# Value tiles with the tokens stationary, convolutions read from the accumulator banks, and modulation steps in other turns

## The reference

```python
h = modulate(layer_norm(x), sh1, sc1)            # sh1, sc1, ... from silu(cond) @ w_ada + b_ada
proj = h @ p['w_in']                             # columns: pool 512 | q 512 | k 512 | v 512 | o 512 | gates 16
qk = silu(dwconv1d_centred(concat([q, k]), w_qk_conv))   # x[t-1]*w0 + x[t]*w1 + x[t+1]*w2, per column
h_f, h_b = mlstm_chunkwise(...)                  # needs q, k by columns and v by tokens
pool_out = pool_mixer(xp, w_pool, pool_scale)    # window means over the grid, then a 128x128 product per group
mix = concat([pool_out, ml_out]) @ p['w_out']
```

## Time and profile before

| | |
|---|---|
| median of three runs | 1317.82 us |
| the profiled execution | 1317.26 us, its span 1315.5 us |
| TensorE busy | 1261.0 us (96%) |
| VectorE / GpSimd busy | 1035.2 us / 668.4 us |
| mean granted TensorE clock | 0.994 of full speed |
| units 4 to 31 | 88.1 to 289.8 us of the span |

### The profile page before, as it was taken

How to read it: one execution, slowest core, us unless ns; L and a number is a source line. 1 busy time by engine, 2 the same in 40 slices (tenths; PEclk the granted TensorE clock), 3 DMA queues, 4 the chain that set the end, 5 groups by cost and what they waited for, 6 DMA issues and landing times.

```text
span 1315.5 us, 21778 instructions
## 1 busy us (share of the span) xinstructions
PE 1261.0 (96%) x7739; PEld 1156.9 (88%) x7739; DVE 1035.2 (79%) x1506; ACT 592.9 (45%) x1029; POOL 668.4 (51%) x503
## 2 busy tenths in 40 slices
PE   6999999999998899989999999999999999999996
PEld 2589999999987778888999999999999988888885
DVE  6455899894567688879887878787875779888898
ACT  5732224545445734555444444444443455345430
POOL 1001999744343011329888888788877874200011
PEclk9999999999999999999999999999999999999999
DMA  9532332473225532203363535444543679945892
GB/s 359 157 88 84 90 94 67 136 240 81 81 81 192 192 113 97 80 33 106 99 204 129 175 120 196 137 160 141 179 147 133 199 238 366 355 134 188 293 322 108
DMA packets 164851, 210.28 MB, mean 160 GB/s; under 512 B 10567, under 2 KB 102819, under 8 KB 164515
## 3 DMA queue, kind: packets, MB, share of 16 engines
q1 hardware_dynamic: 164286, 204.47, 47.4%
q0 software_dynamic: 288, 4.72, 0.9%
q10 hardware_dynamic: 197, 0.06, 0.0%
HBM read 161.49 MB, written 47.72 MB: 159 GB/s over the span
## 4 chain that ended last, share of the span: by engine, by line
PE 51%; POOL 2%; DVE 1%; issue 1%; ACT 0%; POOLq 0%
PE ps L1609 11%; PE ps L1607 11%; PE ps L1608 11%; PE ps L1640 6%; PE ps L1642 6%; PE ps L1641 6%; POOL tlo L2264 0%; POOL ulo L2264 0%; POOL xlo L2264 0%; POOL dwlo L2264 0%; POOL xwlo L2264 0%; PE ps L1166 0%; POOL wsum L2465 0%; DVE z L3275 0%; DVE z L3274 0%
## 5 line engine op out<-in xcount | busy, mean ns | idle before, releaser
L3089 DVE SCALAR_TENSOR_TENSOR ps<-gs,taps,ps 128x945 f32<-128x945 f32 (+2 forms) x176 | 215.7, 1226 | 10.0 <-ACT ps L2042 4.6
L2407 POOL TENSOR_TENSOR rstd<-mv,neghalf 128x1 f32<-128x1 f32 x27 | 25.1, 928 | 258.2 <-DVE mv L3266 156.9
L1259 PE MATMUL ps<-h1hi,whi 128*128 128x384 f32 x432 | 152.9, 354 | 2.7 <-DVE wlo L2603 2.7
L1259 PE MATMUL ps<-h1lo,whi 128*128 128x384 f32 x432 | 145.2, 336 | 0.0
L1259 PE MATMUL ps<-h1hi,wlo 128*128 128x384 f32 x432 | 145.1, 336 | 0.0
L1640 PE MATMUL ps<-dwhi,uhi 128*128 128x512 f32 x290 | 113.1, 390 | 1.3 <-POOL dwlo L2264 1.3
L1642 PE MATMUL ps<-dwhi,ulo 128*128 128x512 f32 x290 | 112.9, 389 | 0.0
L1641 PE MATMUL ps<-dwlo,uhi 128*128 128x512 f32 x290 | 112.8, 389 | 0.0
L1607 PE MATMUL ps<-thi,xhi 128*128 128x288 f32 x320 | 94.3, 295 | 2.0 <-issue 1.1
L2264 POOL TENSOR_TENSOR wlo<-raw,whi 128x512 fp32r<-128x512 f32 x44 | 61.9, 1408 | 65.4 <-ACT whi L1712 29.7
L1609 PE MATMUL ps<-thi,wlo 128*128 128x288 f32 x320 | 94.4, 295 | 0.0
(11 more groups left out here) (444 smaller groups left out, 3998.8 us busy)
## 6 DMA issues: line engine op xcount, KB each, us to landing
raw<-in_w_up SPq DMA_DIRECT2D x78, 256.0 KB, 4.7
u_rows<-val SPq DMA_DIRECT2D x22, 576.0 KB, 2.9
adaw<-in_w_ada SPq DMA_DIRECT2D x24, 512.0 KB, 4.0
st<-in_w_down SPq DMA_DIRECT2D x22, 512.0 KB, 4.3
t_rows<-st SPq DMA_DIRECT2D x11, 1024.0 KB, 4.6
raw<-in_w_in SPq DMA_DIRECT2D x40, 256.0 KB, 4.4
w_raw<-in_w_down SPq DMA_DIRECT2D x33, 256.0 KB, 5.3
v_raw<-u_rows SPq DMA_DIRECT2D x33, 256.0 KB, 4.8
```

The source lines that it names most:

```text
L1259: last = mm(ps[:, bank, 0:GN], a[:, n % 2, k * P:(k + 1) * P], b[:, kk, grp(g)], start=(kk == 0 and a is whi and b is h1hi), stop=(kk == K ...
L2407: tt(rstd[:, j % 4, :], mv[:, j % 4, 1:2], neghalf[:, 0, :], ALU.pow).then_inc(rstd_ready, 1)
L3089: step(stt(a3[:, ro, co], g3[:, ri, ci], taps[:, tap:tap + 1], a3[:, ro, co], ALU.mult, ALU.add), 2 + m)
```

## The change

- **Value tiles.** Units 8 to 15 are replaced by nine `v_tile`s, one for each chunk of 128 tokens. The token chunk is now the stationary operand and the 512 value columns move: 24 matmuls of 128x512 for each tile, in one bank. The result has tokens on its partitions, so the transposes are gone, and ScalarE's `v_evac` copies 9 tiles of 512 columns. Unit 8+k is now the 128 input rows k of the value weights. All eight have to be split before the first value tile can end, into buffers of their own (`vw`), so their loads, `hi` and `lo` are moved ahead, into turns 4 to 8. `lo(16)` and `lo(17)` are made in turn 10.
- **Convolutions.** ScalarE makes only the scaled copy into `qk`. VectorE reads the two outer taps' input straight from the banks. A convolution is in two halves of four instructions, half 0 in odd turns and half 1 in the even turn after it. From unit 20 on TensorE waits for `conv_done` (both halves) before it begins the tile that takes these banks.
- **Modulation steps** are spread differently over the turns: from turn 7 to 15 there are 17 instead of 13, in turns 20 to 23 one each instead of none, in turns 24 to 30 ten instead of eighteen. The third and later `ada2_cols` come three units behind their last step instead of two.

The diff, cut to its core (the memory places of `vw`, counts of `tile_out` and the regrouping of `jobs_after` are left out):

```diff
+V_FIRST, V_LAST = 2 * H, 4 * H
+LO_TURN = {4: (6,), 5: (7,), 6: (8, 9, 10), 7: (11, 12, 13), 8: (14, 15), 10: (16, 17)}
 ...
-ADA_UNITS = {4: 2, 6: 2, 7: 1, 8: 1, 9: 2, 10: 2, 11: 1, 12: 2, 13: 1, 14: 2, 15: 1, 16: 2, 17: 1, 18: 1, 19: 1,
-             24: 2, 25: 3, 26: 3, 27: 3, 28: 3, 29: 3, 30: 1}
+ADA_UNITS = {4: 2, 6: 2, 7: 2, 8: 1, 9: 2, 10: 2, 11: 2, 12: 2, 13: 2, 14: 2, 15: 2, 16: 2, 17: 1, 18: 1, 19: 1,
+             20: 1, 21: 1, 22: 1, 23: 1, 24: 1, 25: 1, 26: 2, 27: 2, 28: 2, 29: 1, 30: 1}
 ...
-ADA_COLS = {min(...) + 2: j for j in range(N_ADA2)}
-for _n in range(12):
-    JOBS[10 + _n] = ("v", _n // 3, _n % 3)
+ADA_COLS = {min(...) + (2 if j < ADA_SIDE[0] - 1 else 3): j for j in range(N_ADA2)}
 ...
# SyncE: loads
+                if V_FIRST <= n < V_LAST:
+                    k = n - V_FIRST
+                    sp.dma_start(raw[:, n % RAWN, :], w_in[0, k * P:(k + 1) * P, 3 * H * P:4 * H * P]).then_inc(raw_in[n % RAWN], 16)
+                    return
 ...
-                if n + RAWN < U_OUT:
-                    load_proj(n + RAWN)
+                for unit in {4: (8,), 5: (9, 10), 6: (11, 12), 7: (13, 14, 15), 8: (16, 17), 9: (18, 19)}.get(n, () if RAWN < n < V_LAST else (n + RAWN,)):
+                    if unit < U_OUT:
+                        load_proj(unit)
 ...
# TensorE: value tiles in place of units 8 to 15
-            def misc_job(job):
-                _, h, part = job
-                ...
-                    last = nc.tensor.transpose(ps[:, 7, (ck % 4) * P:(ck % 4 + 1) * P], qk[:, h, chunk(ck)], ident[:, :])
+            def v_tile(t, between=None):
+                if t == 0:
+                    pe.wait_ge(tile_out, tile_count(2))
+                elif t == NG:
+                    pe.wait_ge(tile_out, tile_count(3))
+                elif t >= 2 * NG:
+                    pe.wait_ge(v_ready, t - 2 * NG + 1)
+                for k in range(KT):
+                    if t == 0:
+                        wait_lo(pe, V_FIRST + k)
+                    w_hi, w_lo = [x[:, :] for x in vw[k]]
+                    for a, w in ((h1hi, w_hi), (h1hi, w_lo), (h1lo, w_hi)):
+                        last = mm(ps[:, t % (2 * NG), :], a[:, k, chunk(t)], w,
+                                  start=(k == 0 and a is h1hi and w is w_hi), stop=(k == KT - 1 and a is h1lo))
+                    if t == NT - 1:
+                        last.then_inc(pe_unit, 1)
+                    if between is not None and k in (2, 5):
+                        between(k // 3)
+                if t < NT - 1:
+                    last.then_inc(pe_v, 1)
 ...
             for n in range(4, 2 * NPROJ):
                 tile, bank = n // 2, 3 * ((n // 2) % 2)
+                if V_FIRST <= n < V_LAST:
+                    v_tile(n - V_FIRST, lambda g: jobs_after(n, g))
+                    jobs_after(n, NG - 1)
+                    if n == V_LAST - 1:
+                        v_tile(NT - 1)
+                    continue
                 wait_lo(pe, n)
-                if n % 2 == 0:
-                    pe.wait_ge(tile_out, tile - 1)
+                if n % 2 == 0 and n > V_LAST + 2:
+                    pe.wait_ge(conv_done, tile - 2 * H - 1)
 ...
# ScalarE
+            def v_evac(t):
+                ...
+                fn(v1[:, t, :, 0:P], ps[:, t % (2 * NG), :].rearrange("p (h n) -> p h n", h=H), ACT.Copy).then_inc(v_ready, 1)
 ...
-                hi(n + 2)
+                if n < V_FIRST - 2:
+                    hi(n + 2)
+                elif n < V_FIRST:
+                    for unit in LO_TURN[n] + ((14, 15) if n == 7 else ()):
+                        v_hi(unit)
 ...
-                        fn(qk[:, j, :]..., ps[:, b0:b0 + 3, 0:GN], ACT.Copy, scale=...)
-                    fn(dst..., ps[:, b0:b0 + 3, 0:GN], ACT.Copy).then_inc(tile_out, 1)
+                    dst, scale = (qk[:, H + tile, :], 1.0) if tile < H else (qk[:, j, :], colv[:, V_CONV + KT + j:V_CONV + KT + j + 1])
+                    fn(dst..., ps[:, b0:b0 + 3, 0:GN], ACT.Copy, scale=scale).then_inc(tile_out, 1)
 ...
# VectorE
-            def conv(j):
-                src, dst = work[:, tile % 2, :], qk[:, j, :]
-                ...
-                        last = stt(dst[:, o], src[:, i_], w[a], dst[:, o], ALU.mult, ALU.add)
+            def conv(j, half):
+                tile = 2 * H + j
+                b0 = 3 * (tile % 2)
+                dst, cut = qk[:, j, :].rearrange("p (g n) -> p g n", g=NG), LAT - 2 * GN
+                if half == 0:
+                    dve.wait_ge(tile_out, tile_count(tile))
+                ...
+                for out, src in ((dst[:, 0:2, to:to + GN - 1], ps[:, b0:b0 + 2, at:at + GN - 1]),
+                                 (dst[:, 2, to:to + cut - 1], ps[:, b0 + 2, at:at + cut - 1]),
+                                 (dst[:, 2, cut + to:GN - 1 + to], ps[:, b0 + 2, cut + at:GN - 1 + at]), joints):
+                    last = stt(out, src, w, out, ALU.mult, ALU.add)
+                if half == 0:
+                    link(last)
                 else:
+                    last.then_inc(conv_done, 1)
 ...
-                if n + 2 < U_LO:
-                    lo(n + 2)
+                for unit in LO_TURN.get(n, () if n < V_LAST else (n + 2,)):
+                    if unit < U_LO:
+                        lo(unit)
 ...
-                if n % 2 == 0 and n // 2 > 2 * H:
-                    conv(n // 2 - 1 - 2 * H)
-            conv(2 * H - 1)
+                if n > V_LAST:
+                    conv((n - 1) // 2 - 2 * H, (n + 1) % 2)
+            conv(2 * H - 1, 1)
```

More of the change, by code:

```diff
@@ L106 @@
 assert ada_done(2 * NPROJ) == N_ADA2 * KT
-ADA_COLS = {min(n for n in range(3, 2 * NPROJ) if ada_done(n) >= KT * (j + 1)) + 2: j for j in range(N_ADA2)}
-for _n in range(12):
-    JOBS[10 + _n] = ("v", _n // 3, _n % 3)
+ADA_COLS = {min(n for n in range(3, 2 * NPROJ) if ada_done(n) >= KT * (j + 1)) + (2 if j < ADA_SIDE[0] - 1 else 3): j
+            for j in range(N_ADA2)}
 POOL_FIRST = 24
@@ L344, in first_split, with tile_count @@
             return wearly[:, 2 * n - 4, :], wearly[:, 2 * n - 3, :]
+        vw = [(place(f"vwhi{k}", [P, UC], at, F32R), place(f"vwlo{k}", [P, UC], at + 4 * UC, F32R))
+              for k, at in enumerate([qk_at + 8 * UC * k for k in range(4)] + [work_at + 1024 + 8 * UC * k for k in range(2)])]
+        late_at = work_at + 4 * 2 * T + 4 * H * P
+        vw += [(place("vwhi6", [P, UC], late_at, F32R), place("vwlo6", [P, UC], late_at + 4 * UC, F32R)),
+               (place("vwhi7", [P, UC], late_at + 8 * UC, F32R), place("vwlo7", [P, UC], past_gates, F32R))]
+        assert late_at + 12 * UC <= work_at + 16 * T and past_gates + 4 * UC <= M0
+        assert 16 * UC * 2 <= 4 * H * T and 1024 + 16 * UC <= 8 * T
+        def tile_count(tile):
+            return tile + 1 if tile < H else tile + 1 - H
         def xslot(n):
@@ L1283, in gate_job @@
                     mm(ps[:, 7, 3 * P:4 * P], bc(gcol[:, 4:5], [P, P]), ident[:, :], start=True, stop=True).then_inc(pe_tok, 1)
-            def misc_job(job):
-                _, h, part = job
[L1288 to L1292, removed]
-                    last = nc.tensor.transpose(ps[:, 7, (ck % 4) * P:(ck % 4 + 1) * P], qk[:, h, chunk(ck)], ident[:, :])
-                last.then_inc(pe_v, 1)
-                jobs_done["v"] += 1
+            def v_tile(t, between=None):
[18 more added lines that the diff above has]
+                    last.then_inc(pe_v, 1)
             def pool_job(j):
                 g, part = divmod(j, 3)
-                pe.wait_ge(v_ready, 13)
+                pe.wait_ge(tok_ready, 1)
                 pe.wait_ge(wpl_in, 16)
@@ L1307, in _, with jobs_after @@
             gate_transposes()
+            def jobs_after(n, g):
+                if g == 1 and n in ADA_COLS:
+                    if n > POOL_FIRST:
+                        pe.wait_ge(po_ready, min(2 * (n - POOL_FIRST), 12))
+                    ada2_cols(ADA_COLS[n])
+                if (n, g) in GATE_JOBS:
+                    gate_job(GATE_JOBS[n, g])
             for n in range(4, 2 * NPROJ):
                 tile, bank = n // 2, 3 * ((n // 2) % 2)
+                if V_FIRST <= n < V_LAST:
[4 more added lines that the diff above has]
+                    continue
                 wait_lo(pe, n)
-                if n % 2 == 0:
-                    pe.wait_ge(tile_out, tile - 1)
+                if n % 2 == 0 and n > V_LAST + 2:
+                    pe.wait_ge(conv_done, tile - 2 * H - 1)
+                elif n == V_FIRST - 2 or n == V_FIRST - 4:
+                    pe.wait_ge(tile_out, tile_count(tile - 2))
                 for g in range(NG):
+                    if n == V_LAST:
+                        pe.wait_ge(v_ready, 2 * NG + g + 1)
                     last = proj_group(n, bank + g, g)
@@ L1316, in _ @@
                         last.then_inc(pe_unit, 1)
[L1317 to L1322 removed]
+                    jobs_after(n, g)
                     if g == 0 and POOL_FIRST <= n < POOL_LAST:
```

(8 more changed lines are left out.)

92 lines of the change are left out of this document (39 added, 53 removed).

## The result

The changed kernel takes 1334.32 us (median of 4 runs, 1332.77 to 1335.77), the one before 1318.0 beside it: a ratio of 1.0124, interval 1.0108 to 1.0141. The forecast was 1321.5, the range ended at 1326. The direction was the likelier one, the size four times too small (+3.8 against +16.3).

What follows compares the result with a forecast made beforehand. It took TensorE, busy for 96% of the span, as the bound. Terms +4.6 + 1.6 - 1.8 - 0.6 = +3.8 us on the profiled 1317.26 gave 1321.1, forecast as a 1321.5 us median; range 1311.5 to 1326.

Steps and rivals of the forecast that it cites:

- the likelier one: Whole kernel: slower by more than 2.6 us, chance 0.42, against 0.32 for faster and 0.26 for within that.
- -0.8 us (1.6 - 1.8 - 0.6): After unit 20: 1.6 us new waits at units 22 and 24, less 1.8 old waits and 0.6 transposing jobs gone.
- part 4: TensorE's new wait for VectorE's queue: unit 20 starts 4.6 us later, waits of 0.8 before units 22 and 24.
- sign that the prediction named for being wrong: In the projection: unit 20 starting before 200 us, or TensorE's waits there summing to less than 5 us.
- Part 1: Value units on TensorE: 0.9 us gained by 512-column matmuls, 4.3 by dropped transposes, together 5.2 us (3.4 to 5.2).
- Part 2: First value tile: TensorE waits about 1.0 us (0 to 4) for the last splits of the value weights.
- Rival D: First value tile: colliding loads delay the splits, a 4 us wait; 1315.4 or 1324.5 us, chance 0.06.
- Part 3: VectorE's convolutions from the banks: 1.75 us a half (1.6 to 1.9), not stretched by GpSimd.
- Rival C: Convolutions: GpSimd still holds instructions with one SBUF operand; about +9 us, 1330, chance 0.04.
- the 4.2 us more that were estimated from that page: Convolutions: bank reads' larger fixed cost, 65 ns on each of 64 VectorE instructions; estimated, not used in the sum.
- the upper price: VectorE beside GpSimd's longest instructions, 199 to 213 us: 2.01 us an instruction, used for the last five before unit 20.
- It decides from 1.38 us downward: Before unit 20: if VectorE's 39 held instructions average 1.38 us instead of 1.54, TensorE's wait there is gone.
- rival A: Projection: VectorE keeps pace, unit 20 starts at 197.1; -5.4 us, 1312.4, chance 0.27.

Runs made afterwards that it cites:

- e2: The changed kernel, but with VectorE's convolutions reading ScalarE's copy in SBUF and TensorE waiting for that copy as before: 1331.66 us, ratio 1.0100.
- e5: The changed kernel with both convolution halves right behind their turn's low part and no modulation step in turns 17 to 21: 1310.61 us, ratio 0.9946.
- e3: The kernel before with only the convolutions read from the banks and one ScalarE copy less: 1321.02 us, ratio 1.0024.
- e8: The changed kernel with each GpSimd window-mean instruction of 900 elements or more given out as two halves: 1316.09 us, ratio 0.9990.
- e1: The changed kernel with the old turns of the modulation units and columns: 1322.83 us, ratio 1.0054.
- e9: The changed kernel with the old modulation turns and both convolution halves ahead of their turn's modulation step: 1315.68 us, ratio 0.9988.
- e4: The changed kernel with GpSimd's window means left out, a tiny fill standing in for each: 1309.72 us, ratio 0.9955.
- e7: The kernel before with only the new value tiles; old modulation turns, convolutions from ScalarE's SBUF copy: 1316.83 us, ratio 0.9999.
- e6: The changed kernel with 30, 40 and 10 unused matmuls on TensorE ahead of the waits of units 18, 20 and 22: 1334.36 us, ratio 1.0121.
- e10: The kernel before with only the new turns of the modulation units: 1335.00 us, ratio 1.0147.

## Why the prediction was wrong, step by step

Forecast and measured, stretch by stretch of the profiled executions: unit 20 starts 4.6 us later (forecast) and 12.5 us later (measured, both counted from 88 us); from there to the scores -0.8 us (1.6 - 1.8 - 0.6) and +1.1. The other 2 of the 15.5 us (0.55 ahead of 88 us, 1.4 behind the scores) belong to no term. So the step that failed is part 4, what stands in VectorE's queue ahead of unit 20 and what it costs. Neither sign that the prediction named for being wrong appeared (unit 20 started at 213.2, TensorE's waits summed to 15.5 us): both guarded only against a loss smaller than forecast.

- **Part 1, TensorE's work: right within its bounds.** 27 matmuls of 512 columns take 6.24 us (147.65 to 153.89), 0.231 us each between the bounds of 0.227 and 0.235. At that pitch 216 of them take 49.9 us, as the eight units did, so the 0.9 us taken as gained for them are none.

```profile
147.65 0.40 PE L1314 MATMUL ps<-vwhi,h1lo 128*128 128x512 f32 x1
...
153.89 0.39 PE L1314 MATMUL ps<-vwhi,h1lo 128*128 128x512 f32 x1
```

- **Part 2, the first value tile: no wait.** It was forecast at 1.0 us, and none of the value tiles' matmuls has a wait in TensorE's list. TensorE started 0.3 us later than forecast (117.69), and 90 matmuls took 0.4 us more than at 0.227. So it is partly luck that VectorE's idling ended at 141.78 where the forecast had 141.7. Rival D fell.
- **Part 3, the convolutions: right.** 1.79 us (forecast 1.75, 1.6 to 1.9) at every place, beside GpSimd and without it. Rival C fell. The Trainium skill (SBUF — State Buffer, Who interferes with whom) states its rule for instructions with at most one SBUF input outside the 2-port perf modes, a condition that the prediction left out. For the convolutions e2 and e5 agree with it: a whole one took 7.23 us from SBUF and 3.61 from the banks. For the first instructions of a block the condition matters (last section). The Trainium skill's rule for a copy first (VectorE: DVE Perf Modes, Rules for kernel authors) holds here only without GpSimd. A whole convolution took 3.13 us from SBUF then (e2, from 309.21) and 3.6 from the banks, though the latter has eight instructions for four; beside GpSimd it took 7.2 to 12.2 us from SBUF against 3.6. In e3 VectorE spent 32.5 us on all convolutions, where it had spent 46.1, and not the 4.2 us more that were estimated from that page.
- **Part 4, who waits: the mechanism right, the term mis-sized. This is the step that failed.** The 39 held instructions were priced at 61.2 us, and took 67.7 (the queue's 71.3 from 141.78 to 213.10, less 3.6 for two halves). The 1.54 us of the earlier trace rows were a mean over a mixture; the 2.01 us, the upper price, were a mean over seven instructions of which four were a convolution from SBUF (8.98 us) and only two modulation instructions. By kinds, from 141.5 to 206 us in the kernel before:

```profile
L2774 DVE SCALAR_TENSOR_TENSOR aacc<-adaw,colv,aacc 128x512 f32<-128x512 f32 x14 | 24.6, 1794 | 0.1
L2774 DVE SCALAR_TENSOR_TENSOR aacc_side<-adaw,colv,aacc_side 128x512 f32<-128x512 f32 x8 | 15.4, 1964 | 0.0
L2603 DVE TENSOR_TENSOR wlo<-raw,whi 128x512 fp32r<-128x512 f32 x8 | 9.1, 1136 | 3.0 <-ACT whi L1712 2.7
L2772 DVE TENSOR_SCALAR aacc_side<-adaw,colv 128x512 f32<-128x512 f32 x2 | 3.0, 1538 | 0.0
L2772 DVE TENSOR_SCALAR aacc<-adaw,colv 128x512 f32<-128x512 f32 x2 | 0.9, 506 | 2.6 <-PE ps L1166 2.6
```

  The modulation's accumulating instructions cost 1.82 us there, and 1.84 in the changed kernel (51.64 / 28); the low parts 1.14, and 1.40; the first instructions of a block 0.98, and 1.52. By kinds the sum would have been 28 x 1.82 + 5 x 1.14 + 6 x 0.98 = 62.5. Of the other 5.2 us 3.2 are in the six first instructions (three of the four before passed at about 0.5 us, one of these six did), 1.3 in the low parts and 0.7 in the accumulating ones: a kind has no fixed price either, it depends on what GpSimd runs beside each. Further, the queue held two halves, and the sum counted one: 1.8 us. 6.5 + 1.8 + 0.1 (the queue began 0.1 late) are 8.4 of the 8.5 by which unit 20 came later than 204.7.
- **The clock: not in the sum.** A wait was priced by its length, and the half clock behind it stood at nothing without a reason. The half clock behind the long one in front of unit 20 adds 1.6 us. Unit 22's wait was 2.40 against 0.8; unit 24's didn't come.
- **"It decides from 1.38 us downward" (rival A)** was a fair mark for unit 20: in e8 the mean was 1.25 us, and the wait before unit 20 was gone (0.10 us). The time fell to that of before and not to rival A's 1312.4, since 2.31 us of waiting came before unit 22.
- **The frame: wrong.** The prediction took the price of a held instruction as a number of the mixture and its count as the lever. e1 against e9 shows the same modulation turns with VectorE's work in another order: 7 to 9 us. The chance of 0.27 on rival A had nothing for it in the rows by kinds, which give 62.5 / 39 = 1.60 us.

## What to carry to other kernels

Price an instruction that another engine holds by its own kind and by what runs beside it at its own place, not by the mean of a stretch; then ask which instruction the other engine waits for, and what stands directly ahead of it in the queue while the holder's longest instruction runs. Where a wait is moved to a new semaphore, put the work that signals it first in its turn and the work that nobody waits for behind. A long instruction of the holder can be given out in pieces, if the holder has time to spare: in e8 GpSimd's run took 118.4 us (124.3 to 242.7) instead of 108.8 (124.4 to 233.2), and TensorE didn't wait for it.

## What was not expected of the hardware

- A VectorE instruction with two SBUF operands took 0.73 us at the least and 0.75 in the mean without GpSimd's run (e4); beside it two took 8.27 (e1). With GpSimd's instructions halved the mean fell from 1964 to 1336 ns. GpSimd's 4.40 us instruction became 2.12 + 2.57 in e8.
- Two operands in SBUF aren't the whole of it. The first instructions of a block read one SBUF tensor and a number per partition; they took 0.48 us each without GpSimd's run (e4) and 1.52 beside it, and even a GpSimd memset held them, of which the prediction had said that it holds nothing up. A modulation instruction with two SBUF operands passed a memset unheld. Both in the changed kernel, each above the memset that ran beside it:

```profile
142.76 1.59 DVE L2827 TENSOR_SCALAR aacc<-adaw,colv 128x512 f32<-128x512 f32 x1
142.62 1.45 POOL L2375 MEMSET poolB<- 128x1424 f32 x1
...
170.89 0.75 DVE L2829 SCALAR_TENSOR_TENSOR aacc<-adaw,colv,aacc 128x512 f32<-128x512 f32 x1
170.37 1.29 POOL L2375 MEMSET poolA<- 128x1424 f32 x1
```

- TensorE's granted clock fell to 1.2 GHz at idle times of 4.37 (e7), 5.77, 7.32 and 10.15 us (e1), 2.71 (e2), 2.75 (e6) and 2.53 (e9), and in e10 at 4.10, 5.63 and even 1.79 us (a mean of 0.57 from 168 to 172 us); at 2.40 in the changed kernel, 2.31 in e8 and 1.82 in e3 it stayed at 2.4. So the length of one idle time doesn't decide it. It can fall during the wait (at 189.0 us, before unit 18 of the changed kernel began) or 0.9 to 1.4 us after work has begun again (e6, e9, twice in e10), so the row just behind a wait doesn't show it. What exactly sets it stays open.
- Low parts were held less than modulation instructions of the same size (1.14 to 1.40 against 1.8 us). In the kernel before one took 0.69 us right behind a held instruction (213.19) and one beside a memset (175.66). No run tells why the others pass so often.
